# Every projection of a hybrid decoder block with the activations still in TensorE and 512 weight columns moving, two k-tiles a chunk

## The chip, the cores and the metric

One core of a Trainium2 chip. The metric is the device time of one execution in microseconds (us), median of three runs. The inputs are float32 in HBM, batch 1, 256 positions.

## The reference, cut to what matters

```python
u = rmsnorm(x, norm_w)                                   # (256, 4096)
proj = u @ w_in                                          # (4096, 24576)
(a_q, a_f, a_i, a_g, c_b, c_c, c_h, c_g, g_a, g_b) = split(proj)   # eight of 2048, two of 4096
f = lb + (1 - lb) * sigmoid(a_f);  k = 1 - f
o_a = rmsnorm(hgrn2(a_q, log(f), k, a_i), hgrn_norm_w)   # 16 heads of 128, linear recurrence
y_a = o_a * silu(a_g)
y_b = c_b * conv3(c_c * c_h) * silu(c_g)                 # causal, depthwise, 3 taps
merged = (sigmoid(g_a + bias_a) * (y_a @ w_branch_a)     # (2048, 4096)
          + sigmoid(g_b + bias_b) * (y_b @ w_branch_b))  # (2048, 4096)
out = rmsnorm(x + merged @ w_out, final_norm_w)          # (4096, 4096)
```

## The kernel before

**Arithmetic.** Each float32 operand of a projection is split in two: a high part (the value rounded to the type fp32r) and a low part (the rest). A product is high x high + high x low + low x high, summed in PSUM. The activations lie in `U` (`[128, 32 k-tiles, 256 high | 256 low]`), the branch outputs in `Y` in the same form.

**A unit of work** in this document is one k-tile (128 rows of a weight matrix) by 256 weight columns, for all 256 positions. There are 4096: 3072 for `w_in`, 512 for the two branch matrices, 512 for `w_out`. A unit is 1536 moving columns on TensorE, in both kernels.

**Two forms.** `channels` (L864) holds the weights still: for each of two 128-column blocks one matmul moves 512 columns (high and low activations against the high weights) and one moves 256 (high activations against the low weights). The result has channels on partitions. `positions` (L877, through `split_product`, L853) holds the activations still: for each of two blocks of 128 positions one matmul moves 256 weight columns (low activations, high weights) and one moves 512 (high activations, high and low weights). The result has positions on partitions. A unit is four matmuls and four weight loads in either form. `positions` serves the a_i group of the recurrence and `w_out`; all else is in `channels`.

**The chunk.** Weights come in chunks of 512 KB, four k-tiles by 256 columns, 1024 in all, 4 units each. Each passes SP (`load`, L225: one DMA into `RAW`), ScalarE (`hi`, L317, the instruction on L321: high part), VectorE (`lo`, L499, L501: low part) and TensorE. `RAW` and the split weights are rings of four. A load waits until the low part of the chunk four before is written; `hi` waits for its DMA and until TensorE has used the chunk four before (`w_used`); `lo` waits for `hi`; TensorE waits for `lo` (`lo_ready`). The split ring is placed at an offset in a 256-byte period that differs by stage: 192 bytes for the recurrence, 0 for the convolution, 128 for the merge, 64 for the output (`AT_...`); `U` lies at 0 and `Y` at 128.

**A group** is one output of 256 columns (eight chunks, or four for a branch matrix), into one of two double banks `PS0`, `PS1`. When it is done ScalarE copies the small halves out of PSUM (`small_half`, L323), VectorE adds them to the big halves (`drain_group`, L552) and multiplies by the 1/rms of x, which `x_rms` (L517) computes during the first group and a matmul with `ONES` (L948) spreads over the free axis. Group n+2 waits for the drain of group n.

**The order.** Eight recurrence iterations of four groups (a_f, a_q, a_i, a_g, two heads each), eight convolution iterations of four groups, sixteen merge iterations (g_a, g_b, z_a, z_b), sixteen output groups. The recurrence of iteration a runs in sixteen hand-written slots among the weight chunks of iteration a+1 (`attention`, on TensorE L886 with the level products on L906). The first group also transposes x (`turn_x`, L840, the instruction on L847: eight transposes before each chunk after the first) and makes `U` from it (L339, L508). The last group runs its last four chunks first for positions 0 to 127, then for 128 to 255, so that the final norm of the one half lies beside the other.

Of the kernel before, what the change touches and what calls it, by code (L numbers as in the profile page):

```python
# [18 lines left out]
KC = 4  # L41
# [3 lines left out]
NG = D // GW  # L45
XW = KC * P
XC = 1024
PERIOD = 256
AT_Y = 128
AT_HGRN, AT_CONV, AT_MERGE, AT_OUT = 192, 0, 128, 64  # L50
EARLY = 2
SLOTS = 16
# [3 lines left out]
A_Q, A_F, A_I, A_G, C_B, C_C, C_H, C_G = (BW * n for n in range(8))  # L56
G_A, G_B = 8 * BW, 8 * BW + D
HGRN_GROUPS = (A_F, A_Q, A_I, A_G)
CONV_GROUPS = (C_G, C_C, C_H, C_B)
X_AHEAD = ((4, 5), (6,), (7,), ())  # L60

TURNS_BRANCH = 4 * CD // RING
TURNS_MERGE = (2 * CD + 2 * CB) // RING
TURNS_OUT = 2 * CD // RING
CONV_TURN = NP * TURNS_BRANCH
MERGE_TURN = 2 * CONV_TURN
OUT_TURN = MERGE_TURN + NG * TURNS_MERGE
CONV_GROUP = 4 * NP
MERGE_GROUP = 2 * CONV_GROUP
OUT_GROUP = MERGE_GROUP + 4 * NG  # L70


def build(nc, x, norm_w, w_in, lb_logits, hgrn_norm_w, conv_w, w_branch_a, w_branch_b,
          gate_bias, w_out, final_norm_w, out):
    ctx = ExitStack()
    with ctx:
# [6 lines left out]
        def sem(name):  # L83
# [5 lines left out]
        region_y = region_u + KT * 2 * T * 4 + AT_Y  # L89
        region_m = region_y + 2 * KB * 2 * T * 4  # L90
# [6 lines left out]
        XR = at("XR", [P, 2, D], region_y + 2 * D * 4)  # L97
        MRG = at("MRG", [P, KT, T], region_m)
# [5 lines left out]
        ONES = at("ONES", [P, P], region_m + 8 * XW + 8 * P)  # L104
        VEC0 = at("VEC0", [KT, P], region_m + 8 * XW + 12 * P)
        W2 = 2 * T
        names = ["F", "V", "G", "SF", "SG", "PRE", "K", "SUF"]
        F, V, G, SF, SG, PRE, K, SUF = [at(n, [P, W2], region_m + 4 * W2 * i)
                                        for i, n in enumerate(names)]

        QX = at("QX", [P, 4, 192], region_m + 4 * W2 * len(names))
        QC = at("QC", [P, W2], region_m + 4 * W2 * len(names))
        scr = region_m + 4 * W2 * len(names) + 16 * 192
# [7 lines left out]
        RAW = [sb(f"RAW{i}", [P, KC, GW]) for i in range(RING)]  # L121
        ring = (nc.sbuf_base + PERIOD - 1) // PERIOD * PERIOD
        slot = KC * 2 * GW * 4 + PERIOD
        ctx.enter_context(nc.sbuf_tensor("ring", [P, (ring + RING * slot - nc.sbuf_base + 3) // 4], F32))

        def slots(stage, first):

            return [at(f"W{stage}{i}", [P, KC, 2 * GW], ring + i * slot + first, F32R) for i in range(RING)]

        W_HGRN, W_CONV = slots("H", AT_HGRN), slots("C", AT_CONV)  # L130
        W_MERGE, W_OUT = slots("M", AT_MERGE), slots("O", AT_OUT)
        SM = [sb(f"SM{i}", [P, 2, T]) for i in range(2)]
        GA, GB, Z = [sb(n, [P, W2]) for n in ("GA", "GB", "Z")]
        MASK = Z[:, 0:6 * 64]
        IDN = sb("IDN", [P, P])
        RB = sb("RB", [P, T])
        NW = GB[:, 64:64 + KT]
        VT1 = sb("VT1", [P, 96])
# [3 lines left out]
        LT = GB[:, 0:48]  # L142
        SSQ = sb("SSQ", [P, 2, NG])
# [5 lines left out]
        PS = [ctx.enter_context(nc.psum_tensor(f"PS{i}", [P, 2, 512], F32)) for i in range(2)]  # L149
# [8 lines left out]
        EPS_WRITTEN, IDN_WRITTEN, N_CONSTS = 1, 3, 19  # L158
# [6 lines left out]
        small_out = sem("small_out")  # L165
        drained = sem("drained")
        x_loaded = [sem(f"x_loaded{i}") for i in range(CD)]
# [8 lines left out]
        x_rstd = sem("x_rstd")  # L176
        x_spread = sem("x_spread")
# [6 lines left out]
        u_ready = sem("u_ready")  # L184
        gate_f = sem("gate_f")
        gate_g = sem("gate_g")
        level_ready = sem("level_ready")
# [6 lines left out]
        y_ready = sem("y_ready")  # L194
        merge_gate = sem("merge_gate")
        merged = sem("merged")
        m_hi = sem("m_hi")
        m_ready = sem("m_ready")
        xr_loaded = [sem(f"xr_loaded{i}") for i in range(2)]
        h_ready = sem("h_ready")  # L200
# [12 lines left out]

        block = ctx.enter_context(nc.Block())
# [3 lines left out]
        def _(sp):  # L218
# [12 lines left out]
            def column(i, col):  # L231


                return i * GW + col if col else (i + 1) * GW - GW

            def load_vectors():
                sp.dma_start(VEC1[0:32, :], lb_logits.rearrange("a (k p) -> (a k) p", p=P)).then_inc(vec_loaded, 16)
                sp.dma_start(VEC1[32:96, :], gate_bias.rearrange("a b (k p) -> (a b k) p", p=P)).then_inc(vec_loaded, 16)
# [3 lines left out]
            def branch(i, cols, turn0, first=False):  # L242
                for n, col in enumerate(cols):
                    col = column(i, col)
                    for c in range(CD):
                        if first and n == 0:
                            for j in ((c,) if c < RING else X_AHEAD[c - RING]):
                                load_x(j)
                            if c == CD - 1:
                                load_vectors()  # L250
                        load(w_in[0], c, col, turn0 + TURNS_BRANCH * i + (n * CD + c) // RING, c % RING,
                             free=not (first and n == 0 and c < RING))

            branch(0, HGRN_GROUPS, 0, first=True)
            with sp.Fori(1, NP) as i:
                branch(i, HGRN_GROUPS, 0)
            with sp.Fori(0, NP) as i:
                branch(i, CONV_GROUPS, CONV_TURN)
            with sp.Fori(0, NG) as i:
                turn = MERGE_TURN + TURNS_MERGE * i  # L260
                for n, col in enumerate((G_A, G_B)):
                    col = column(i, col)
                    for c in range(CD):
                        load(w_in[0], c, col, turn + (n * CD + c) // RING, c % RING)
                col = column(i, 0)
                for n, w in enumerate((w_branch_a, w_branch_b)):
                    for c in range(CB):
                        load(w[0], c, col, turn + (2 * CD + n * CB + c) // RING, c % RING)

            with sp.Fori(0, NG // 2) as i:  # L270
                for n in range(2):
                    col = column(i * 2 + n, 0)
                    for c in range(CD):
                        load(w_out[0], c, col, OUT_TURN + TURNS_OUT * i + (n * CD + c) // RING, c % RING)
                    if n == 0:
                        sp.wait_ge(w_used, RING * OUT_TURN)
                        sp.wait_ge(m_ready, CD)
                    cols = bass.ds(col, GW)
# [10 lines left out]
        def _(pool):  # L289
# [6 lines left out]
            pool.memset(ONES[:, :], 1.0).then_inc(consts, 1)  # L296
            pool.memset(AD[:, :, :], 0.0).then_inc(consts, 1)
            pool.memset(KL[:, :, :], 0.0).then_inc(consts, 1)
            pool.wait_ge(consts, 7)

            for n, m in enumerate(LEVELS[:6]):
# [3 lines left out]
                pool.wait_ge(consts, 8 + 2 * n)  # L305
# [6 lines left out]
        def _(act):  # L312
# [4 lines left out]
            def hi(ws, turn, s, free=True):  # L317
                act.wait_ge(raw_loaded[s], turn * 16 + 16)
                if free:
                    act.wait_ge(w_used, RING * turn + s - (RING - 1))  # L320
                act.activation(ws[s][:, :, 0:GW], RAW[s][:, :, :], ACT.Copy).then_inc(hi_ready, 1)  # L321

            def small_half(group, chunks, par, free=True, positions=False):  # L323
                act.wait_ge(w_used, chunks)
                if free:
                    act.wait_ge(drained, group - 1)
                if positions:
                    for b in range(2):
                        op = act.activation(SM[par][:, b, :], PS[par][:, b, T:2 * T], ACT.Copy, scale=ST[:, 12 + b:13 + b])
                    op.then_inc(small_out, 1)  # L330
                else:
                    act.activation(SM[par][:, :, :], PS[par][:, :, T:2 * T], ACT.Copy).then_inc(small_out, 1)

            act.wait_ge(gain_out, 1)
            for c in range(CD):

                for k in range(KC * c, KC * (c + 1)):
                    act.wait_ge(x_turned, k + 1)
                    act.activation(U[:, k, 0:T], XB[k % len(XB)], ACT.Copy, scale=NW[:, k:k + 1]).then_inc(u_hi, 1)  # L339
                hi(W_HGRN, c // RING, c % RING, free=c >= RING)  # L340

                act.wait_ge(x_loaded[c], 16)
                act.drain()
                act.activation(SQA[:, :], XS[:, 0, c * XW:(c + 1) * XW], ACT.Square,
                               accum_out=SSQ[:, 0, c:c + 1]).then_inc(x_sq, 1)
            def attention(a, slot):
                if slot == 1:

                    act.wait_ge(drained, 4 * a + 4)
                    act.activation(SG[:, :], G[:, :], ACT.Sigmoid).then_inc(gate_g, 1)  # L350
# [18 lines left out]
            def branch(i, turn0, group0, a=None, first=False, is_conv=False, after_it=None):  # L369
                own = W_CONV if is_conv else W_HGRN  # L370

                def ahead(c):

# [641 lines left out]
```

## Time and profile before

| | |
|---|---|
| median of 3 runs | 2955.69 us (2955.37 to 2956.11) |
| the profiled execution | 2955.83 us |
| its span | 2954.1 us |
| TensorE matmul busy | 2935.4 us (99%), 17061 matmuls |
| TensorE weight load busy | 2572.9 us (87%), 17061 loads |
| VectorE, ScalarE, GpSimd busy | 1700.8 us (58%), 1308.3 us (44%), 6.9 us |
| DMA | 552.32 MB, mean 187 GB/s, 60.4% of 16 engines' span |
| granted TensorE clock | 0.999 of full speed |

Busy time of a matmul is from its start to its modelled end, so that neighbours overlap; the spacing of their starts tells what one costs in a stream. In a timeline a row may hold several instructions (x2), with the time from the first's start to the last's end.

### The profile page before, as it was taken

What the parts mean: (1) busy time and instruction counts of PE and PEld (TensorE: products, weight loads), DVE (VectorE), ACT (ScalarE), POOL (GpSimd) and SP (SyncE); (2) the same over time, 40 slices, a digit from 0 to 9 for tenths busy, and PEclk for the clock granted to TensorE, in tenths of its full rate; (3) what the DMA queues carried; (4) which work ended last, traced back from release to release, by engine and by line L of the source; (5) the groups of instructions that cost most, each with busy time, mean ns of one, the idle gap of its engine ahead of it and who ended that gap; (6) DMA issues with size and microseconds to landing.
All of it is one profiled execution on the core that took longest, in us unless ns stands there. A gap on an engine that the chain in (4) does not pass through costs nothing.

```text
span 2954.1 us, 46544 instructions
## 1 busy us (share of the span) xinstructions
PE 2935.4 (99%) x17061; PEld 2572.9 (87%) x17061; DVE 1700.8 (58%) x1973; ACT 1308.3 (44%) x1523; POOL 6.9 (0%) x23
## 2 busy tenths in 40 slices
PE   9999999999999999999999999999999999999998
PEld 7888888888888888888888888888888888888887
DVE  7566665676665555555555555555555555655554
ACT  6444444444444444444444444444444444544444
POOL 0000000000000000000000000000000000000000
PEclk9999999999999999999999999999999999999999
DMA  7555555555556555566566666666666666666665
GB/s 242 180 177 166 171 176 177 165 172 174 173 171 191 187 190 186 179 196 192 186 191 186 190 186 190 185 191 186 190 186 190 186 190 186 189 203 208 202 204 190
DMA packets 550945, 552.32 MB, mean 187 GB/s; under 512 B 17217, under 2 KB 547826, under 8 KB 550898
## 3 DMA queue, kind: packets, MB, share of 16 engines
q1 hardware_dynamic: 550898, 551.71, 60.4%
q8 instruction: 27, 0.44, 0.1%
q14 instruction: 20, 0.16, 0.0%
HBM read 547.45 MB, written 4.19 MB: 187 GB/s over the span
## 4 chain that ended last, share of the span: by engine, by line
PE 99%; DMA 0%; DVE 0%; ACT 0%; issue 0%; ACTq 0%; SPq 0%; DVEq 0%
PE PS L869 52%; PE PS L872 26%; PE PS L861 12%; PE PS L856 6%; PE SC L906 1%; DMA XS<-in_x 0%; PE SS L906 0%; PE OB L915 0%; PE OB L916 0%; PE SC L896 0%; PE OB L914 0%; PE SS L921 0%; PE PS L847 0%; PE SC L847 0%; PE OB L847 0%
## 5 line engine op out<-in xcount | busy, mean ns | idle before, releaser
L501 DVE TENSOR_TENSOR WM<-RAW,WM 128x1024 fp32r<-128x1024 f32 x384 | 470.4, 1225 | 489.1 <-ACT WM L321 475.4
L321 ACT ACTIVATE WM<-RAW 128x1024 fp32r<-128x1024 f32 x384 | 407.5, 1061 | 605.1 <-PE PS L872 605.1
L869 PE MATMUL PS<-U,WC 128*128 128x512 f32 x2048 | 644.0, 396 | 0.0
L869 PE MATMUL PS<-U,WM 128*128 128x512 f32 x2048 | 638.0, 393 | 0.0
L869 PE MATMUL PS<-U,WH 128*128 128x512 f32 x1536 | 483.8, 396 | 0.5 <-DVE WH L501 0.5
L501 DVE TENSOR_TENSOR WC<-RAW,WC 128x1024 fp32r<-128x1024 f32 x256 | 312.2, 1225 | 282.9 <-ACT WC L321 273.7
L872 PEld LDWEIGHTS PS<-U,WC 128*128 128x128 f32 x2048 | 384.7, 188 | 90.9
L872 PEld LDWEIGHTS PS<-U,WM 128*128 128x128 f32 x2048 | 384.5, 188 | 89.2
L321 ACT ACTIVATE WC<-RAW 128x1024 fp32r<-128x1024 f32 x256 | 271.4, 1060 | 409.2 <-PE PS L872 409.2
L321 ACT ACTIVATE WH<-RAW 128x1024 fp32r<-128x1024 f32 x256 | 271.8, 1062 | 401.1 <-PE PS L872 273.4
L501 DVE TENSOR_TENSOR WH<-RAW,WH 128x1024 fp32r<-128x1024 f32 x256 | 311.6, 1224 | 227.8 <-ACT WH L321 217.4
L872 PE MATMUL PS<-U,WM 128*128 128x256 f32 x2048 | 406.1, 279 | 0.0
L872 PE MATMUL PS<-U,WC 128*128 128x256 f32 x2048 | 402.4, 278 | 0.0
L861 PE MATMUL PS<-WO,U 128*128 128x512 f32 x1024 | 359.1, 395 | 0.0
L872 PEld LDWEIGHTS PS<-U,WH 128*128 128x128 f32 x1536 | 289.0, 188 | 64.6
L869 PE MATMUL PS<-Y,WM 128*128 128x512 f32 x1024 | 321.4, 395 | 0.0
L869 PEld LDWEIGHTS PS<-U,WM 128*128 128x128 f32 x2048 | 312.8, 188 | 0.0
L869 PEld LDWEIGHTS PS<-U,WC 128*128 128x128 f32 x2048 | 311.8, 189 | 0.1
L872 PE MATMUL PS<-U,WH 128*128 128x256 f32 x1536 | 304.1, 279 | 0.0
L856 PE MATMUL PS<-WO,U 128*128 128x256 f32 x1024 | 285.5, 281 | 0.0
L501 DVE TENSOR_TENSOR WO<-RAW,WO 128x1024 fp32r<-128x1024 f32 x128 | 155.3, 1224 | 157.8 <-ACT WO L321 157.7
L869 PEld LDWEIGHTS PS<-U,WH 128*128 128x128 f32 x1536 | 234.5, 189 | 1.1 <-issue 0.7
(179 smaller groups left out, 2523.6 us busy)
## 6 DMA issues: line engine op xcount, KB each, us to landing
RAW<-in_w_in SPq DMA_DIRECT2D x768, 512.0 KB, 3.7
RAW<-in_w_out SPq DMA_DIRECT2D x128, 512.0 KB, 3.8
RAW<-in_w_branch_a SPq DMA_DIRECT2D x64, 512.0 KB, 3.7
RAW<-in_w_branch_b SPq DMA_DIRECT2D x64, 512.0 KB, 3.7
XS<-in_x SPq DMA_DIRECT2D x8, 512.0 KB, 9.7
XR<-in_x SPq DMA_DIRECT2D x16, 256.0 KB, 4.0
out_dram<-H SPq DMA_DIRECT2D x8, 512.0 KB, 4.0
FW<-in_final_norm_w SPq DMA_DIRECT2D x16, 128.0 KB, 3.8
```

The source lines that it names most:

```text
L321: act.activation(ws[s][:, :, 0:GW], RAW[s][:, :, :], ACT.Copy).then_inc(hi_ready, 1)
L501: dve.tensor_tensor(ws[s][:, :, GW:2 * GW], RAW[s][:, :, :], ws[s][:, :, 0:GW], ALU.subtract).then_inc(lo_ready, 1)
L856: return pe.matmul(bank[:, T:2 * T], stat_lo, both[:, 0:T], start=False, stop=stop, skip_group_check=True)
L861: op = pe.matmul(bank, stat_hi, both, start=first, stop=last, skip_group_check=True)
L869: pe.matmul(PS[par][:, t, :], w[:, k, t * P:(t + 1) * P], rhs[:, at_k, :], start=at_k == 0, stop=False, skip_group_check=True)
L872: op = pe.matmul(PS[par][:, t, T:2 * T], w[:, k, GW + t * P:GW + (t + 1) * P], rhs[:, at_k, 0:T], start=False, stop=at_k == n_tiles - 1, s ...
L906: op = pe.matmul(out, k_side, q_side, start=True, stop=True)
```

## The change

All projections take one form, `product`: the activations of 128 positions are still (`top` the high part, `low` the low part) and 512 weight columns move. One k-tile by 512 columns is six matmuls of 512 columns, three for each block of positions, and six weight loads. A chunk is two k-tiles by 512 columns: still 512 KB and 4 units, still 1024 chunks. In the branches its 512 columns are two blocks of 256 from two column groups (a_q and a_f, a_i and a_g; c_b and c_g, c_c and c_h), loaded by two DMAs of 256 KB. Groups are twice as wide: 2 in place of 4 in a branch iteration, 8 merge iterations and 8 output groups in place of 16.

Every result has positions on partitions. So 1/rms is one number for each partition (the `ONES` matmul, `RB` and `small_half` go), the merge biases are loaded by DMA broadcast to all partitions (`BIAS`), and what is needed with channels on partitions is transposed on TensorE: f and q after chunk 24 of each recurrence iteration (`turn_fq`), the gate product and c_c x c_h after chunk 2 of the next convolution iteration (`turn_conv`), and the merged output after chunk 3 of the next merge iteration (`turn_merged`), eight 128x128 transposes each, 192 in all. The ring of split weights lies at offset 0 of the period in all stages, with no padding between slots; so do `U` and `Y`.

```diff
-KC = 4
+OW = 512
+KC = 2
...
+FQ_AT, CONV_AT, MERGED_AT = 24, 2, 3
...
-            def load(w, rows, col, turn, s, free=True):
-                src = w[rows * KC * P:(rows + 1) * KC * P, bass.ds(col, GW)]
+            def load_pair(blocks, i, c, chunk, free=True):
+                s = c % RING
+                src = w_in[0][rows(c), 0:8 * BW].rearrange("(k p) (g c) -> p k g c", p=P, c=BW)
+                src = src[:, :, blocks, bass.ds((i + 1) * GW - GW, GW)]
                 if free:
-                    sp.wait_ge(lo_ready, RING * turn + s - (RING - 1))
-                sp.dma_start(RAW[s][:, :, :], src.rearrange("(k p) c -> p k c", p=P)).then_inc(raw_loaded[s], 16)
+                    sp.wait_ge(lo_ready, chunk - (RING - 1))
+                dst = RAW[s][:, :, :].rearrange("p k (g c) -> p k g c", g=2)
+                for k in range(KC):
+                    sp.dma_start(dst[:, k, :, :], src[:, k, :, :]).then_inc(raw_loaded[s], 16)
...
+            def load_bias(n, i):
+                cols = bass.ds((i + 1) * OW - OW, OW)
+                sp.dma_start(BIAS[:, :], gate_bias[0, n, cols].partition_broadcast(P)).then_inc(bias_loaded, 16)
...
-            def channels(par, w, rhs, k0, n_tiles):
-                for k in range(KC):
-                    at_k = k0 + k
-                    for t in range(2):
-                        pe.matmul(PS[par][:, t, :], w[:, k, t * P:(t + 1) * P], rhs[:, at_k, :],
-                                  start=at_k == 0, stop=False, skip_group_check=True)
-                    for t in range(2):
-                        op = pe.matmul(PS[par][:, t, T:2 * T], w[:, k, GW + t * P:GW + (t + 1) * P],
-                                       rhs[:, at_k, 0:T], start=False, stop=at_k == n_tiles - 1,
-                                       skip_group_check=True)
+            def product(par, s, left, k0, n_tiles, halves=(0, 1)):
+                w = WS[s]
+                for k in range(KC):
+                    at_k = k0 + k
+                    for b in halves:
+                        top, low = left[:, at_k, b * P:(b + 1) * P], left[:, at_k, T + b * P:T + (b + 1) * P]
+                        bank = PS[par][:, b, :]
+                        pe.matmul(bank, top, w[:, k, 0:OW], start=at_k == 0, stop=False)
+                        pe.matmul(bank, top, w[:, k, OW:2 * OW], start=False, stop=False)
+                        op = pe.matmul(bank, low, w[:, k, 0:OW], start=False, stop=at_k == n_tiles - 1)
                 return op
...
+            def turn_fq(i, first):
+                pe.wait_ge(drained, 2 * i + 1)
+                if first:
+                    pe.wait_ge(lb_ready, 1)
+                blocks = [GA[:, b, h * P:(h + 1) * P] for h in range(4) for b in range(2)]
+                for g in range(4):
+                    pe.transpose(SC[1][:, g * P:(g + 1) * P], blocks[g], IDN[:, :])
+                turn(SC[0], blocks[4:], fq_turned)
+            def turn_conv(a):
+                pe.wait_ge(drained, CONV_GROUP + 2 * a + 2)
...
+            def turn_merged(i):
+                pe.wait_ge(merged, i + 1)
...
-            def drain_group(dst, group, par, norm=None):
...
+            def scaled(dst, src):
+                for b in range(2):
+                    op = dve.tensor_scalar(dst[:, b, :], src[:, b, :], inv_rms(b), None, ALU.mult)
+                return op
...
                     if c == 2 * CD + CB - 1:
+                        dve.wait_ge(w_used, chunk + c + 1)
+                        dve.wait_ge(merge_gate, 2 * i + 1)
+                        dve.tensor_tensor(GA[:, :, :], PS[0][:, :, :], GA[:, :, :], ALU.mult).then_inc(drained, 1)
+                dve.wait_ge(w_used, chunk + MERGE)
+                dve.wait_ge(merge_gate, 2 * i + 2)
+                dve.tensor_tensor(GB[:, :, :], PS[1][:, :, :], GB[:, :, :], ALU.mult).then_inc(drained, 1)
+                after()
+                dve.tensor_tensor(GA[:, :, :], GA[:, :, :], GB[:, :, :], ALU.add).then_inc(merged, 1)
```

## Rows read from the trace of the kernel before

**Rows 1.** The page: busy time of each engine, and the granted clock in 40 slices
```profile
PE 2935.4 (99%) x17061; PEld 2572.9 (87%) x17061; DVE 1700.8 (58%) x1973; ACT 1308.3 (44%) x1523; POOL 6.9 (0%) x23
...
PEclk9999999999999999999999999999999999999999
```

**Rows 2.** The page: the chain that ended last, by engine, shares of the span
```profile
PE 99%; DMA 0%; DVE 0%; ACT 0%; issue 0%; ACTq 0%; SPq 0%; DVEq 0%
```

**Rows 3.** Waits: engine, line, who was waited for: total us, times, longest
```profile
ACT WM L321 <- PE PS L872: 605.1, 383, 2.0
DVE WM L501 <- ACT WM L321: 475.4, 319, 1.8
...
SPq L229 <- DVE WM L501: 839.9, 384, 5.6
```

**Rows 4.** Windows, TensorE alone, in convolution, merge, output: stretch, length, busy (matmuls), clock
```profile
900.00:1470.00 570.00, 570.00 (x3275) 1.00 0.60 189
1490.00:2570.00 1080.00, 1080.00 (x6201) 1.00 0.62 188
2590.00:2930.00 340.00, 340.00 (x1936) 1.00 0.67 204
```

**Rows 5.** Timeline of TensorE in a recurrence iteration, channels form: start, us, instructions
```profile
85.64 0.62 PE L869 MATMUL PS<-U,WH 128*128 128x512 f32 x2
...
88.40 0.39 PE L869 MATMUL PS<-U,WH 128*128 128x512 f32 x1
```

**Rows 6.** Timeline of TensorE, positions form, in a recurrence iteration
```profile
171.85 0.40 PE L861 MATMUL PS<-WH,U 128*128 128x512 f32 x1
172.08 0.28 PE L856 MATMUL PS<-WH,U 128*128 128x256 f32 x1
172.20 0.40 PE L861 MATMUL PS<-WH,U 128*128 128x512 f32 x1
...
173.26 0.40 PE L861 MATMUL PS<-WH,U 128*128 128x512 f32 x1
```

**Rows 7.** The same form in the output stage
```profile
2637.94 0.39 PE L861 MATMUL PS<-WO,U 128*128 128x512 f32 x1
...
2639.33 0.40 PE L861 MATMUL PS<-WO,U 128*128 128x512 f32 x1
```

**Rows 8.** Groups by line: weight loads; timeline: two of them side by side
```profile
L872 PEld LDWEIGHTS PS<-U,WC 128*128 128x128 f32 x2048 | 384.7, 188 | 90.9
```
```profile
86.22 0.30 PEld L869 LDWEIGHTS PS<-U,WH 128*128 128x128 f32 x2
```

**Rows 9.** Timeline of TensorE in the first group: one chunk with eight transposes of x
```profile
15.38 0.71 PE L869 MATMUL PS<-U,WH 128*128 128x512 f32 x2
...
19.04 0.70 PE L869 MATMUL PS<-U,WH 128*128 128x512 f32 x2
```

**Rows 10.** Groups by line on VectorE and ScalarE: busy, mean ns of one, idle before
```profile
L501 DVE TENSOR_TENSOR WM<-RAW,WM 128x1024 fp32r<-128x1024 f32 x384 | 470.4, 1225 | 489.1 <-ACT WM L321 475.4 <-issue 9.7
L321 ACT ACTIVATE WM<-RAW 128x1024 fp32r<-128x1024 f32 x384 | 407.5, 1061 | 605.1 <-PE PS L872 605.1
...
L332 ACT ACTIVATE SM<-PS 128x512 f32<-128x512 f32 x135 | 78.1, 579 | 0.0
L565 DVE TENSOR_TENSOR SM<-PS,SM 128x512 f32<-128x512 f32 x88 | 60.6, 689 | 10.6 <-issue 7.4 <-ACT SM L332 2.0
```

**Rows 11.** Timeline of the first 50 us: making of U, a stall, the ONES matmul
```profile
6.88 0.90 ACT L339 ACTIVATE U<-SC,GB 128x256 fp32r<-128x256 f32 x2
```
```profile
37.18 0.70 PE L869 MATMUL PS<-U,WH 128*128 128x512 f32 x2 [0.53 <-DVE WH L501]
```
```profile
45.92 0.70 PE L948 MATMUL SC<-GA,ONES 128*128 128x256 f32 x2
```

**Rows 12.** Timeline of VectorE behind the last matmul
```profile
2942.96 0.42 DVE L815 TENSOR_TENSOR GB<-PS,SM 128x256 f32<-128x256 f32 x1
2943.89 0.42 DVE L817 CUSTOM_DVE_ANT_0 SM<-GB 128x256 f32<-128x256 f32 x1 [0.50 <-issue]
```

**Rows 13.** The page, DMA issues: count, KB each, us to landing
```profile
RAW<-in_w_in SPq DMA_DIRECT2D x768, 512.0 KB, 3.7
```

More of the change, by code:

```diff
@@ L315, in _, with hi @@
             act.activation(ST[:, 19:20], EPT[:, :], ACT.Sqrt)
-            def hi(ws, turn, s, free=True):
-                act.wait_ge(raw_loaded[s], turn * 16 + 16)
+            def hi(chunk, s, free=True):
+                act.wait_ge(raw_loaded[s], (chunk - s) * (16 * KC // RING) + 16 * KC)
                 if free:
[L320 to L332, printed above, removed]
+                    act.wait_ge(w_used, chunk - (RING - 1))
+                act.activation(WS[s][:, :, 0:OW], RAW[s][:, :, :], ACT.Copy).then_inc(hi_ready, 1)
             act.wait_ge(gain_out, 1)
@@ L399, in branch @@
                         gates(i)
-                    if slot % 4 == 3:
-                        n = slot // 4
-                        small_half(group0 + 4 * i + n, RING * (turn0 + TURNS_BRANCH * i) + CD * (n + 1), n % 2, free=not (first and n < 2), positions=n == 2 and not is_conv)
-            branch(0, 0, 0, first=True)
-            with act.Fori(1, NP - 1) as i:
-                branch(i, 0, 0, a=i - 1)
-            branch(NP - 1, 0, 0, a=NP - 2, after_it=W_CONV)
-            branch(0, CONV_TURN, CONV_GROUP, a=NP - 1, is_conv=True)
@@ new lines, in branch @@
+                    if is_conv and slot == 15:
+                        act.wait_ge(w_used, chunk0 + BRANCH * i + 2 * CD)
+                        act.wait_ge(drained, CONV_GROUP + 2 * i + 1)
+                        for b in range(2):
+                            op = act.activation(pair(SF)[:, b, :], PS[1][:, b, 0:T], ACT.Copy, scale=inv_rms(b))
+                        op.then_inc(gate_c, 1)
+            branch(0, 0, first=True)
+            with act.Fori(1, NP) as i:
+                branch(i, 0, a=i - 1)
@@ new lines, in _, with merge @@
+            branch(0, CONV_CHUNK, a=NP - 1, is_conv=True)
+            with act.Fori(1, NP) as i:
+                branch(i, CONV_CHUNK, is_conv=True)
+            def merge(i, first=False, last=False):
+                chunk = MERGE_CHUNK + MERGE * i
+                group = MERGE_GROUP + 4 * i
+                for c in range(MERGE):
+                    hi(chunk + c + RING, c % RING)
+                    if not first and c == MERGED_AT + 2:
+                        act.wait_ge(m_turned, i)
+                        for j in range(2):
+                            op = act.activation(MRG[:, bass.ds(i * 4 + 2 * j - 4, 2), :], pair(SC[j]), ACT.Copy)
+                        op.then_inc(m_kept, 1)
+                    if c in (CD + 1, 2 * CD + 1):
@@ L950, in branch @@
-            def branch(i, turn0, group0, modes, a=None, first=False):
-                for n in range(4):
-                    group(W_HGRN if turn0 == 0 else W_CONV, turn0 + TURNS_BRANCH * i, n * CD, CD, modes[n], U, 0, n % 2, group0 + 4 * i + n,
-                          free=not (first and n < 2), u_wait=(u_ready, KC) if first and n == 0 else None, a=a)
-            hgrn = (channels, channels, positions, channels)
-            branch(0, 0, 0, hgrn, first=True)
+                    pe.wait_ge(lo_ready, chunk0 + at_chunk + 1)
@@ new lines, in group, with branch, between @@
+                    product(par, at_chunk % RING, left[:, k_start:k_start + n_chunks * KC, :], c * KC,
+                            n_chunks * KC).then_inc(w_used, 1)
+                    between(at_chunk)
+            def branch(i, chunk0, group0, a=None, first=False, is_conv=False, conv_of=None):
+                def between(c):
+                    if a is not None:
+                        attention(a, c)
+                    if first and c == CD + 1:
+                        turn_vectors()
+                    if not is_conv and c == FQ_AT:
+                        turn_fq(i, first)
+                    if conv_of is not None and c == CONV_AT:
+                        turn_conv(conv_of)
+                for n in range(2):
+                    group(chunk0 + BRANCH * i, n * CD, CD, U, 0, n, group0 + 2 * i + n, between,
+                          free=not first, x_first=first and n == 0)
@@ new lines, in merge, with between @@
+            def merge(i, first=False):
+                def between(c):
+                    if first and c == CONV_AT:
+                        turn_conv(NP - 1)
+                    if not first and c == MERGED_AT:
+                        turn_merged(i - 1)
+                chunk0, g = MERGE_CHUNK + MERGE * i, MERGE_GROUP + 4 * i
+                group(chunk0, 0, CD, U, 0, 0, g, between)
+                group(chunk0, CD, CD, U, 0, 1, g + 1, between)
+                pe.wait_ge(y_ready, 2 * NP)
+                group(chunk0, 2 * CD, CB, Y, 0, 0, g + 2, between)
+                group(chunk0, 2 * CD + CB, CB, Y, KB, 1, g + 3, between)
@@ L970, in output @@
+            merge(0, first=True)
+            with pe.Fori(1, NM) as i:
+                merge(i)
             def output(i, first=False, last=False):
                 for n in range(1 if last else 2):
-                    group(W_OUT, OUT_TURN + TURNS_OUT * i, n * CD, CD, positions, U, 0, n, OUT_GROUP + 2 * i + n,
-                          u_wait=(m_ready, 1) if first and n == 0 else None)
+                    pe.wait_ge(drained, OUT_GROUP + 2 * i + n - 1)
+                    for c in range(CD):
+                        if first and n == 0 and c % 2 == 0:
+                            pe.wait_ge(m_ready, c // 2 + 1)
+                        at_chunk = OUT_CHUNK + 2 * CD * i + n * CD + c
+                        pe.wait_ge(lo_ready, at_chunk + 1)
+                        product(n, c % RING, U, c * KC, KT).then_inc(w_used, 1)
+                        if first and n == 0 and c == MERGED_AT:
+                            pe.wait_ge(m_kept, NM - 1)
+                            turn_merged(NM - 1)
```

620 lines of the change are left out of this document (290 added, 330 removed).

## The prediction

> **What bounds the kernel now.** I read the page first: TensorE is busy for 99% of the span at full clock, VectorE for 58%, ScalarE for 44% [rows 1]. A matmul's end is modelled, so 99% alone proves little. The chain that ended last says more: 99% of it is TensorE [rows 2]. The waits then show that everything else waits for TensorE: in the merge stage ScalarE waits 605.1 us until TensorE frees a slot of split weights, VectorE 475.4 us for ScalarE, SP 839.9 us for VectorE [rows 3]. Preparation follows the matmuls; it doesn't hold them up. So the question is how closely matmul starts follow one another.
>
> A unit (one k-tile by 256 weight columns) is 1536 moving columns; at one column a cycle of the granted 2.4 GHz it would take 640 ns. Four matmuls make a unit, so the windows give 4 x 570/3275 = 696 ns in the convolution, 4 x 1080/6201 = 697 in the merge, 4 x 340/1936 = 702 in the output stage [rows 4]. Recurrence, weights still: one chunk of four units from 85.64 to 88.40 is 2.76 us, 690 ns a unit [rows 5]. Positions form: four pairs (two units) take 1.41 us in the recurrence, 705 a unit [rows 6], and 1.39 us here in the output stage, 695 [rows 7]. Summed by their numbers: 768 x 0.690 + 256 x 0.705 + 1024 x 0.696 + 1536 x 0.697 + 512 x 0.702 = 2853 us. The other 101 us of the span are the recurrence's own products, the transposes, the start, small waits and the tail.
>
> **The stream.** The change removes no moving column: 3 matmuls of 512 in place of two of 512 and two of 256. What can change is the excess of 50 to 65 ns a unit over 640. It has two possible prices. By column, the unit stays as it is: 695 to 705 in the form that holds activations still. By instruction, three quarters of the excess stay: from the positions mean of 702 that is 640 + 0.75 x 62 = 687, from the quickest row, 690, it is 677.5. The single starts lie between the two: a 512 takes 0.23 us (171.85 to 172.08), a 256 takes 0.12 [rows 6], against 0.213 and 0.107 by column count; the excess of a 512 is larger, but not twice as large. No row has three 512s one after another with the same activations still, so this is an estimate with both ends kept: 677.5 to 707 (705 and 2 ns for the rounding of the rows). I take 0.232 us for a 512, 696 ns a unit, because the nearest rows, the positions form, put their 512s at 0.23. Stream: 4096 x 0.696 = 2851, **-2 us**.
>
> The trace has a 256 following in 0.12 us while a weight load lasts 188 ns, two loads side by side fitting into 0.30 us [rows 8]; loads overlap and don't set the spacing, and four loads or three a unit is all one. The Trainium skill, Perfetto Trace Analysis (Identifying the Most-Contended Engine), takes the load's busy share as the better measure of how near TensorE is to its limit; by that rule 87% is the bound and a quarter fewer loads would free time. The trace speaks against it here. The skill's page TensorE: Matmul & The Clock Gate (Wait — 56ns, not 53.3ns?) gives N/2.4 + about 2.5 ns between starts, 215.8 ns for a 512; then a unit would be 650 before and 647.5 after, an estimate of -10 us from fewer instructions. The rows, at 0.23, don't follow it.
>
> **Transposes.** 24 places of eight, on TensorE's path. The price is in the first group: a chunk with eight transposes of x lasts 15.38 to 19.04 = 3.66 us, one without 2.76 [rows 5, 9], so eight cost 0.90. 24 x 0.90 = **+21.6 us**. They can't be hidden, since TensorE is the bound. Bounds: nothing if they run in gaps (there are none), 48 us at twice the price. The transposes of x and the recurrence's products stay.
>
> **Start.** The first product needs two k-tiles of `U` rather than four: one ScalarE pair of 0.90 us less before the first `hi` [rows 11]; I take -0.8. The 0.53 us stall ahead of the eighth chunk goes, since per chunk ScalarE has half the `U` work; the `ONES` matmul goes [rows 11], 0.6 net of the vector transposes that stay. **-1.9 us**. The first group now fetches 12 MB over sixteen chunks where it was 8 MB over eight, but at 3.2 us or more a chunk; the DMA engines are not the limit there.
>
> **Tail.** Behind the last matmul one add of 512 stands for two of 256, and the square sum is 512 wide (0.69 for 0.42) [rows 10, 12]: **+0.2 us**.
>
> **Costed at nothing, with their cover.** Chunk, `hi` and `lo` keep their size: 1061 and 1225 ns in 2.78 us [rows 10]. Between the freeing of a slot and its use there are three chunks, 8.3 us; `hi` and `lo` take 2.3, so 6 us of slack cover what is put among them. The drains: the `small_half` copies (135 x 579 ns) and one add (88 x 689) go [rows 10], wide operations of 1024 elements come, about 1.2 us each; at the end of a merge iteration VectorE does two in a row, 2.5 us, inside the slack. The new waits of TensorE: `turn_merged` comes after four chunks, 11.1 us, and its chain is `hi` and `lo` 2.3 + 2.5 + drains, under 6; `turn_conv` comes after three chunks, 8.3 us, with a chain of `hi`, two ScalarE copies, two VectorE products, under 5; `turn_fq` waits for a group drained eight chunks before. If one were late, every chunk behind it would start late, since TensorE's queue is in order; but the queues behind VectorE and ScalarE still have the slack. DMA: the bytes stay; branch chunks are two issues of 256 KB in place of one. Landing takes 3.7 us [rows 13] and starts when `lo` frees the slot four chunks ahead, so about 5 us remain. The bias loads (16 of 256 KB written) stand in SP's queue behind waits that are long fulfilled. If that cover failed, one chunk would be late by what is missing, seldom over 2 us, in 16 places.
>
> **Sum.** 2954.1 - 2 + 21.6 - 1.9 + 0.2 = 2972 for the span; 1.7 us lie around the span (2955.83 - 2954.1), the profiled execution being within 0.2 of the median: about **2973 us**.
>
> **The rivals.**
> 1. *Fewer instructions pay* (the other side): the excess belongs to the matmul, a 512 takes 0.229 us. Unit 687: 4096 x 0.687 = 2814, -39, +19.9 for the rest: 2936 us; at 677.5 it is 2897. It decides from 692 ns a unit (0.2306 us for a 512), where the stream gains 20 us and pays for the transposes. For it: a 256 carries 12 ns more than its columns, more than half of a 512's. Against: the positions form, nearest to the new one, is the dearest. Chance 0.27.
> 2. *Full rate*: three equal matmuls in a row stream at one column a cycle of 2.4 GHz, unit 640: 2621, -232, +19.9: 2744 us. Against: no stage comes near it. The skill's load measure and its 2.5 ns rule would lead here. Chance 0.04.
> 3. *The dear form everywhere*: all at 705 to 707, as in rows 6, because weights move and `U` is the still operand, or because the ring lies at one offset with `U`: +35 to +43 on the stream, 3010 to 3018 us. For it: the spacing differs by stage (690 to 705) with nothing but form and place of the operands different. Chance 0.22.
> 4. *A turn comes too early* or a drain delays a chunk: 24 places at 1 us, 2997 us. Against: the slack above. Chance 0.07.
>
> My forecast, 0.40: unit of 692 to 701.
>
> **How the numbers follow.** A measurement of this kernel can tell 0.2%, 6 us, from no change. Faster: rivals 1 and 2 and the low edge of the forecast, 0.33. Within 0.2% (units of 691 to 693.5): 0.12. Slower: 0.55. The range leaves out rival 2 and the ends of 1 and 3: 2915 to 3012. Both signs carry weight, so the forecast alone: 2956 to 2993.
>
> **What would show it.** All groups of matmuls are 128x512 but for the recurrence; 12288 of them, starts 0.232 apart; a chunk of 2.78 us in every stage. Three groups of 64 transposes, idle before them near nothing. ScalarE still waits for TensorE, VectorE for ScalarE. The prediction is wrong if a 512 follows in under 0.2306 us (faster), if chunks differ by stage, if TensorE shows idle time before the transposes, or if its waits name a DMA.

## The result and the profile after

| | before | after |
|---|---|---|
| median | 2955.9 us | 2910.4 us (2910.26 to 2911.84) |
| ratio | | 0.9847, interval 0.983 to 0.9864 |
| span of the profiled execution | 2954.1 us | 2908.5 us |
| matmuls, weight loads | 17061 | 13155 |

The change makes the kernel 1.5% faster, 45.5 us. I had forecast 2973 us, slower, with 2915 to 3012 as range: wrong in direction, and just outside the range. (The median before is now that of four runs.)

The page of the changed kernel, busy times, clock and chain, in the form of [rows 1, 2]:

```profile
PE 2889.1 (99%) x13155; PEld 2399.5 (82%) x13155; DVE 1600.1 (55%) x1794; ACT 1231.9 (42%) x1326; POOL 6.7 (0%) x22
...
PEclk9999999999999999999999999999999999999999
...
PE 99%; DVE 0%; ACT 0%; DMA 0%; ACTq 0%; DVEq 0%; issue 0%; SPq 0%
```

TensorE is still the whole chain. Who waits for whom is unchanged too, against [rows 3]:

```profile
ACT WS L314 <- PE PS L839: 1613.6, 957, 3.1
DVE WS L483 <- ACT WS L314: 1226.6, 868, 2.9
...
SPq L222 <- DVE WS L483: 1061.0, 512, 4.3
```

So the gain is in the spacing of matmuls, and the timeline shows it. This is TensorE in the convolution, one matmul a row, start first:

```profile
986.18 0.39 PE L839 MATMUL PS<-WS,U 128*128 128x512 f32 x1
986.41 0.39 PE L837 MATMUL PS<-WS,U 128*128 128x512 f32 x1
986.63 0.39 PE L838 MATMUL PS<-WS,U 128*128 128x512 f32 x1
986.86 0.39 PE L839 MATMUL PS<-WS,U 128*128 128x512 f32 x1
987.09 0.39 PE L837 MATMUL PS<-WS,U 128*128 128x512 f32 x1
987.31 0.39 PE L838 MATMUL PS<-WS,U 128*128 128x512 f32 x1
...
990.03 0.39 PE L838 MATMUL PS<-WS,U 128*128 128x512 f32 x1
```

From 987.31 to 990.03 are twelve matmuls, one chunk of four units: 2.72 us, 0.2267 a matmul, 680 ns a unit. Before, a chunk took 2.76 to 2.82 us, by stage [rows 4 to 7]. The same stretch of the output stage, where nothing else runs on TensorE, counts matmuls, before and then after:

```profile
2660.00:2860.00 200.00, 200.00 (x1140) 1.00 0.68 205
```
```profile
2660.00:2860.00 200.00, 200.00 (x884) 1.00 0.66 212
```

Four of 175 ns make a unit of 702 ns before, three of 226 make 679 after. (A count over 200 us is good to one or two matmuls.)

The turns, here between two chunks of the convolution, with the matmul before and behind:

```profile
888.50 0.39 PE L839 MATMUL PS<-WS,U 128*128 128x512 f32 x1
888.73 0.60 PE L899 MATMUL SC<-IDN,F 128*128 128x128 f32 x4
889.17 0.60 PE L845 MATMUL SC<-IDN,SG 128*128 128x128 f32 x4
889.52 0.48 PE L837 MATMUL PS<-WS,U 128*128 128x512 f32 x1
889.84 0.40 PE L838 MATMUL PS<-WS,U 128*128 128x512 f32 x1
```

No idle time stands before the transposes. They take 0.79 us to the start of the next matmul, and that one is followed after 0.32 in place of 0.23: 0.9 us in all, as forecast.

At the start TensorE now waits before the first product, and later it has two stalls where there was one [rows 11]:

```profile
9.45 0.76 PE L837 MATMUL PS<-WS,U 128*128 128x512 f32 x1 [2.01 <-DVE WS L483]
...
59.31 0.47 PE L837 MATMUL PS<-WS,U 128*128 128x512 f32 x1 [0.23 <-DVE WS L483]
...
62.92 0.51 PE L837 MATMUL PS<-WS,U 128*128 128x512 f32 x1 [0.60 <-DVE WS L483]
```

### The profile page after: what moved, and what is told of

It reads as the page before. It is cut to its first block, busy times and chain, and to the rows that moved or that the text cites. A ratio compares the mean times of both kernels' runs of the same rounds, so it can differ in the third digit from the quotient of the medians.

```text
span 2908.5 us, 39078 instructions
## 1 busy us (share of the span) xinstructions
PE 2889.1 (99%) x13155; PEld 2399.5 (82%) x13155; DVE 1600.1 (55%) x1794; ACT 1231.9 (42%) x1326; POOL 6.7 (0%) x22
## 4 chain that ended last, share of the span: by engine, by line
PE 99%; DVE 0%; ACT 0%; DMA 0%; ACTq 0%; DVEq 0%; issue 0%; SPq 0%
PE PS L837 32%; PE PS L839 32%; PE PS L838 32%; PE SC L868 1%; PE SC L845 0%; PE SS L868 0%; DMA XS<-in_x 0%; DVE WS L483 0%; PE SS L845 0%; PE OB L878 0%; PE OB L877 0%; PE SC L858 0%; PE OB L876 0%; PE SC L899 0%; PE SC L891 0%; PE SC L907 0%
## 5 line engine op out<-in xcount | busy, mean ns | idle before, releaser
L483 DVE TENSOR_TENSOR WS<-RAW,WS 128x1024 fp32r<-128x1024 f32 x1024 | 1253.7, 1225 | 1247.9 <-ACT WS L314 1226.6
L314 ACT ACTIVATE WS<-RAW 128x1024 fp32r<-128x1024 f32 x1024 | 1084.6, 1060 | 1617.4 <-PE PS L839 1613.6
L837 PE MATMUL PS<-WS,U 128*128 128x512 f32 x3584 | 1408.2, 393 | 2.8 <-DVE WS L483 2.8
L839 PE MATMUL PS<-WS,U 128*128 128x512 f32 x3584 | 1397.3, 390 | 0.0
L838 PE MATMUL PS<-WS,U 128*128 128x512 f32 x3584 | 1396.7, 390 | 0.0
L839 PEld LDWEIGHTS PS<-WS,U 128*128 128x128 f32 x3584 | 673.5, 188 | 140.9
L837 PEld LDWEIGHTS PS<-WS,U 128*128 128x128 f32 x3584 | 673.8, 188 | 140.0 <-issue 3.0
L838 PEld LDWEIGHTS PS<-WS,U 128*128 128x128 f32 x3584 | 674.0, 188 | 135.8
L839 PE MATMUL PS<-WS,Y 128*128 128x512 f32 x512 | 199.4, 389 | 0.0
L837 PE MATMUL PS<-WS,Y 128*128 128x512 f32 x512 | 199.4, 389 | 0.0
L838 PE MATMUL PS<-WS,Y 128*128 128x512 f32 x512 | 199.3, 389 | 0.0
L839 PEld LDWEIGHTS PS<-WS,Y 128*128 128x128 f32 x512 | 96.1, 188 | 20.0
L838 PEld LDWEIGHTS PS<-WS,Y 128*128 128x128 f32 x512 | 96.1, 188 | 19.9
L837 PEld LDWEIGHTS PS<-WS,Y 128*128 128x128 f32 x512 | 96.2, 188 | 19.9
L868 PEld LDWEIGHTS SC<-QR,KL 128*126 128x126 f32 (+5 forms) x384 | 42.9, 173 | 6.4 <-issue 2.8
L868 PE MATMUL SC<-QR,KL 128*126 128x64 f32 (+5 forms) x384 | 42.5, 254 | 0.0
L565 DVE TENSOR_TENSOR PRE<-PRE 128x256 f32<-128x256 f32 x56 | 23.9, 426 | 4.6 <-issue 0.5
L553 DVE TENSOR_TENSOR KL<-K,SUF 128x256 f32<-128x256 f32 x56 | 23.3, 416 | 0.0
```

Source lines behind the costliest of these rows:

```text
L314: act.activation(WS[s][:, :, 0:OW], RAW[s][:, :, :], ACT.Copy).then_inc(hi_ready, 1)
L483: dve.tensor_tensor(WS[s][:, :, OW:2 * OW], RAW[s][:, :, :], WS[s][:, :, 0:OW], ALU.subtract).then_inc(lo_ready, 1)
L553: op = dve.tensor_tensor(halves(KL[:, n % 2, :], m)[0], halves(K[:, :], m)[0], s_left, ALU.mult)
L565: dve.tensor_tensor(p_right, p_right, over_left, ALU.mult)
L837: pe.matmul(bank, top, w[:, k, 0:OW], start=at_k == 0, stop=False)
L838: pe.matmul(bank, top, w[:, k, OW:2 * OW], start=False, stop=False)
```

## The experiments

Theories: **I**, a matmul with its weight load costs a constant over its columns; **C**, the excess goes by columns; **R**, a second matmul on the same still operand is cheaper; **P**, the place of the split ring against `U` sets the excess; **M**, neighbours of unequal size cost. The kernel before was timed beside every run; the ratios are to it. e13 was timed once, the others four times or more. No run leaves out any of the work.

### e1: the old mix of sizes in the new form

```diff
-                        op = pe.matmul(bank, low, w[:, k, 0:OW], start=False, stop=at_k == n_tiles - 1)
+                        for c0 in (0, 256):
+                            op = pe.matmul(bank[:, c0:c0 + 256], low, w[:, k, c0:c0 + 256], start=False,
+                                           stop=at_k == n_tiles - 1, skip_group_check=True)
```

> The changed kernel with one edit: the low x high matmul of 512 columns is issued as two of 256, so that a unit is again two matmuls of 512 and two of 256, as before the change. Theory I (the excess over one column a cycle belongs to the matmul with its weight load, 13 ns each): 4096 more matmuls cost 55 us, about 2965 us, a chunk of four units goes from 2.72 to 2.77 us. Theory C (the excess goes by moving columns, and something else in the change, place or order, made the columns cheaper): no change, about 2910 us, chunk 2.72 us.

Measured: 2975.6 us, ratio to before 1.0068 (1.0051 to 1.0084); 65.2 us more than the changed kernel. The timeline in the convolution, and below it the kernel before at the same time:

```profile
1305.51 0.40 PE L843 MATMUL PS<-WS,U 128*128 128x512 f32 x1
1305.74 0.39 PE L844 MATMUL PS<-WS,U 128*128 128x512 f32 x1
1305.97 0.40 PE L839 MATMUL PS<-WS,U 128*128 128x256 f32 x2
1306.20 0.40 PE L843 MATMUL PS<-WS,U 128*128 128x512 f32 x1
...
1307.60 0.40 PE L843 MATMUL PS<-WS,U 128*128 128x512 f32 x1
```
```profile
1306.17 0.63 PE L869 MATMUL PS<-U,WC 128*128 128x512 f32 x2
1306.64 0.39 PE L872 MATMUL PS<-U,WC 128*128 128x256 f32 x2
1306.87 0.40 PE L869 MATMUL PS<-U,WC 128*128 128x512 f32 x1
```

1306.20 to 1307.60 are two units, 0.70 each; before, 1306.17 to 1306.87 is one, 0.70. With the ring at offset 0 the new form with the old sizes runs as the old form did. C falls. This one edit takes back more than the whole gain: the number and size of the matmuls are worth 65 us, and which operand is still shows no price in these rows. Theory I had said 55 us, 13.3 ns for each of the 4096 matmuls more; it was 15.9. So about 10 us of the 65 come with the mixture of sizes and not with the count; no run says why.

### e2: the same still operand not twice in a row

The third and the second matmul of `product` change places.

> The changed kernel with the three matmuls in the order high x high, low x high, high x low, so that no two neighbours hold the same activations still. Theory I: no change, 2910 us, 0.227 us for each matmul. Theory R (a second matmul on the same still operand is cheaper, which the order before the change could not use): the two cheap successions of six go, each costing up to the 4 to 5 ns by which a 512 got cheaper, 12288 x 5 = up to 60 us, about 2970 us.

Measured: 2910.6 us (0.9847, 0.983 to 0.9863). R falls: loading the same operand twice in succession saves nothing.

### e3, e6, e7, e12, e15, e14: the ring moved against U

```diff
-        region_w = region_y + 2 * KB * 2 * T * 4
+        region_w = region_y + 2 * KB * 2 * T * 4 + 64
```

and 128, 192, 32, 96, 256 in the others.

e3, 64 bytes:

> The changed kernel with the ring of split weights, RAW and what lies behind them moved by 64 bytes against U and Y, the offset that the output stage had before the change. Theory I: no change, 2910 us. Theory P (the place of the ring against U sets the excess): the spacing moves from 0.227 towards the 0.230 to 0.235 of the kernel before, 12288 x 3 to 8 ns = 37 to 98 us more, 2947 to 3008 us.

e6, 128 bytes:

> The changed kernel with the ring of split weights 128 bytes off against U in the 256-byte period. Theory P2 (what counts is the place of the moving operand against the still one; 64 bytes cost 6.75 ns a unit, 25.6 us in all): another chunk length than 2.720 and 2.747 us, either way, by up to some 30 us. If the merge stage of before is a guide, where 128 bytes gave 697 ns against 697 at 0, nothing changes: 2910 us.

e7, 192 bytes:

> The changed kernel with the ring 192 bytes off against U. In the recurrence stage of before 192 bytes gave 690 ns a unit against 696.7 at 0 (the run of before with all offsets at 0). Theory P2: a gain of up to 27 us, 2883 us, if the offset works alike in the form with 512 columns alone; no change or a loss if not.

e12, 32 bytes:

> The changed kernel with the ring 32 bytes off against U. At 0, 64, 128, 192 bytes a unit takes 680, 687, 697, 700 ns. On the line between 0 and 64: 683 to 684, 2922 us. If offset 0 is no optimum but one point of a curve, it could fall under 680, to 2900 us or less.

e15, 96 bytes:

> The changed kernel with the ring 96 bytes off against U. Measured: 2910 at 0, 2989 at 32, 2936 at 64, 2979 at 128, 2988 at 192. If 0 and 64 are the two good places and odd multiples of 32 the bad ones: near 2989 us. A time under 2910 would show that 0 is no floor.

e14, 256 bytes:

> The changed kernel with the ring, RAW and what lies behind them 256 bytes further off from U. If the place matters within a period of 256 bytes: 2910 us, chunk 2.720 us. If the distance itself matters: another time, up to the 2989 us of 32 bytes.

| offset, bytes | 0 | 32 | 64 | 96 | 128 | 192 | 256 |
|---|---|---|---|---|---|---|---|
| us | 2910.4 | 2989.2 | 2936.1 | 2988.5 | 2979.3 | 2988.4 | 2911.1 |
| ratio to before | 0.9847 | 1.0112 | 0.9934 | 1.0111 | 1.008 | 1.011 | 0.9849 |

The intervals are about 0.0017 to either side. The stretch 2660 to 2860 us, at 64, 128 and 192 bytes:

```profile
2660.00:2860.00 200.00, 200.00 (x876) 1.00 0.65 207
```
```profile
2660.00:2860.00 200.00, 200.00 (x862) 1.00 0.64 206
```
```profile
2660.00:2860.00 200.00, 200.00 (x859) 1.00 0.64 204
```

884 matmuls at offset 0 become 876, 862 and 859: 0.226, 0.228, 0.232 and 0.233 us each. P holds, and is larger than the whole effect of the change: with the ring 32, 96, 128 or 192 bytes off the new kernel would have been 0.8 to 1.1% slower than the old. 256 is as good as 0, so it is the place within a period that counts. Several expectations were wrong. For 64 bytes I had at least 37 us more, it was 26. For 128 I had up to 30 us either way, it was 69 more; for 192 a gain or some loss, it was 78 more: the old stages at these offsets (697 and 690 ns a unit) were no guide. For 32 bytes I had a line from 0 to 64: the price isn't smooth, and 64 is the cheapest place but 0 of those tried. None of the five other places tried in the period beats 0; 160 and 224 bytes were not tried.

### e9, e10: what against what

```diff
-        base = (nc.sbuf_base + PERIOD - 1) // PERIOD * PERIOD
+        base = (nc.sbuf_base + PERIOD - 1) // PERIOD * PERIOD + 128
```

> The changed kernel with the whole arena 128 bytes further: U, Y, the split ring, RAW and the rest keep their places against one another. If the place of the ring against U counts (relative), 2910 us, chunk 2.720 us. If the ring's own place in the period counts (absolute), as in the run with 128 bytes: 2979 us, chunk 2.79 us.

Measured: 2910.9 us (0.9847, 0.9831 to 0.9863). In e10 the ring alone moves by 128 bytes, and RAW and the scratch return to offset 0:

```diff
+        region_w = region_y + 2 * KB * 2 * T * 4 + 128
+        region_r = region_w + RING * KC * 2 * OW * 4 + 128
```

> The changed kernel with only the split ring 128 bytes off; RAW and all behind it are back at offset 0 of the period. If TensorE's reads of the ring against those of U make the difference, 2979 us, chunk 2.79 us, as with everything behind U and Y moved. If RAW or the scratch against U had done it, 2910 us.

Measured: 2980.9 us (1.0083, 1.0066 to 1.01), as in e6. The place is relative, and it is that of the ring TensorE moves against the `U` and `Y` it holds still.

### e4: the kernel before with all at offset 0

`AT_Y` and all four ring offsets are set to 0.

> The kernel before with the split ring and Y at offset 0 of the 256-byte period in all stages, as after the change. Theory I: the number of matmuls is unchanged, so the time stays within 10 us of 2956. Theory P: it falls by what the change won on the stream, 64 us, to about 2892 us.

Measured: 2955.6 us (1.0, 0.999 to 1.0009). The 2892 us of theory P was wrong. The stages moved against each other. In the recurrence the channels form lost what 192 bytes had given it: this row pair and its distance, four units, is 2.80 us against 2.76 [rows 5].

```profile
86.16 0.64 PE L869 MATMUL PS<-U,WH 128*128 128x512 f32 x2
...
88.96 0.40 PE L869 MATMUL PS<-U,WH 128*128 128x512 f32 x1
```

The output stage won a little (1145 matmuls from 2660 to 2860 us where there were 1140, 699 ns a unit for 702). With the old sizes, then, no gain from offset 0; place and size act together.

### e5 and e13: smaller matmuls

Every matmul but the first of a sum is issued in two of 256 columns, or in four of 128.

> The changed kernel with every projection matmul issued as two of 256 columns (save the first of each sum), six a unit. Theory I (a fixed excess for each matmul with its load): from the mixed run a 256 costs 0.1216 us when a 512 costs 0.2267, so a unit is 6 x 0.1216 = 0.730 us, chunk 2.92 us, 205 us more than the changed kernel: about 3115 us. Theory M (only neighbours of unequal size cost): all are equal again, chunk about 2.72 us, 2910 us.

> The changed kernel with every projection matmul issued as four of 128 columns (save the first of each sum), twelve a unit. By columns plus a constant of 13.3 ns, a matmul of 128 takes 66.7 ns, a unit 800 ns, 4096 x 0.120 = 492 us more than the changed kernel, about 3400 us, plus waits at the loop ends as with 256 columns. If a weight load sets a floor of 120 ns for each matmul, a unit takes 1440 ns, about 6000 us in all.

e5 measured: 3124.6 us (1.0571, 1.0553 to 1.0588). A stretch of it in the merge:

```profile
1800.00:1870.00 70.00, 70.00 (x582) 1.00 0.60 189
```

70/582 = 0.120 us a matmul, 720 ns a unit. From 256 to 512 columns the spacing grows from 120.0 to 226.7 ns: 106.7 ns for 256 columns, one a cycle of 2.4 GHz, with 13.3 ns left over both times. As the cause of the change M falls, since all are equal here and the unit is 40 ns dearer. 4096 x 0.040 = 164 us of the 214 are this. The rest is mostly waits that I hadn't expected, and a lower clock behind them:

```profile
PE PS L844 <- issue: 18.1, 8, 2.4
PE PS L844 <- DVE WS L483: 13.2, 6, 2.8
PE PS L839 <- issue: 10.0, 6, 2.8
```
```profile
1884.50:1888.00 3.50, 3.50 (x18) 0.58 0.58 175
```

Two of these twenty waits are those of the start. The other eighteen, 38 us in all, stand at the turns of the recurrence loop (twelve, two at each turn) and of the merge loop (six), whose bodies have here nearly twice the matmuls; the convolution loop has none. In fourteen of them TensorE waits for nothing that the profile shows. The last row above follows a turn of the merge loop, where TensorE had waited 2.26 us until 1884.33: the granted clock was 0.58 over 3.5 us, and 0.94 over the next four. Over the run the clock is 0.994 where it was 0.999, about 15 us by estimate. The changed kernel has no wait at a loop's turn. Its DMA queue for instructions moved 33 packets, that of e5 182 and that of e13 430 (part 3 of their pages), so the waits may be for the instructions themselves; no run tests that.

e13 gave 7578 us in one run. Its page, with the clock in 40 slices, one wait, and windows before and behind it:

```profile
PE 7518.9 (99%) x49587; PEld 7504.6 (99%) x49587; DVE 1602.7 (21%) x1794; ACT 1234.2 (16%) x1326; POOL 6.7 (0%) x22
...
PEclk9998888889965555555555557998898898997555
```
```profile
2157.61 0.79 PE L844 MATMUL PS<-WS,U 128*128 128x512 f32 x1 [2.90 <-DVE WS L483]
```
```profile
2100.00:2150.00 50.00, 50.00 (x450) 1.00 0.33 103
2200.00:4600.00 2400.00, 2400.00 (x11224) 0.50 0.17 52
4660.00:4700.00 40.00, 40.00 (x360) 1.00 0.34 99
```

The expectation of 6000 us by a floor was near in kind. At full clock, in the 10 us from 949.83 on, 92 matmuls are about 0.112 us apart, far from 0.067. So 128 columns meet a floor of about 0.112 us that isn't their columns. Weight loads are busy for 99% of the span and are the likely cause, but no run changes the loads alone. At 256 columns the loads are busy for 98% too (3050.9 of 3122.2 us in e5); 0.120 lies above the floor, yet so little that a part of its 13.3 ns may belong to the load.

The rest of the time is the clock. From 2200 to 4600 us it is at its lower level, 1.2 GHz, and a matmul takes 0.214 us. After the start TensorE waits fourteen times, 2.5 to 3.1 us each, at loop turns, and the granted clock falls to 0.50 behind each of the fourteen and nowhere else. It came back after 40 to 55 us in twelve cases, after 2500 us in the one shown, and not before the end behind the wait at 6914 us, while TensorE issued without a gap. (From 100 to 400 us the record has the clock at 1.00 and 1403 matmuls, also 0.214 us each, so the record is not to be trusted there.) By estimate some 19,000 matmuls had the slower pace, 0.10 us each: 1900 to 2000 us, which with 48720 x 0.112 us and some 120 us of other work comes near the 7578.

### e11: alternate banks

The six matmuls of a k-tile are ordered high x high for both halves of positions, then high x low, then low x high.

> The changed kernel with the six matmuls of a k-tile ordered so that the two banks alternate: high x high for both halves of positions, then high x low, then low x high. Same matmuls, same sums. If part of the 13.3 ns that each matmul takes over its columns comes from following in the same bank, the spacing falls from 0.2267 towards 0.2133, up to 164 us less. If it belongs to the matmul with its load, no change: 2910 us. The still operand now changes at every matmul; the order with the low part in the middle showed that as free.

Measured: 2910.5 us (0.9846, 0.9829 to 0.9862). No part of the 13.3 ns comes from following in the same bank.

### e8: the turns doubled

```diff
+                if done is not o_turned:
+                    for n in range(8):
+                        g = n % 4
+                        op = pe.transpose(bank[:, g * P:(g + 1) * P], blocks[g], IDN[:, :])
                 op.then_inc(done, 1)
```

> The changed kernel with the 24 turns of eight transposes doubled: eight more transposes of blocks already turned, into the same bank, behind the eight. (They overwrite blocks of the second bank with the blocks of that bank's first four, so its contents stay.) If turns lie on TensorE's path at 0.90 us for eight, 24 x 0.87 to 0.90 = 21 to 22 us more, 2932 us. If part of them hides in waits, less; if they disturb the queues of VectorE and ScalarE, more.

Measured: 2931.7 us (0.9916, 0.99 to 0.9933), +21.3 us. The turns lie wholly on TensorE's path.

## Why the prediction was wrong, point by point

- **What bounds the kernel**: right. TensorE is 99% of the chain before and after, and all that stood under "costed at nothing" stayed hidden: no wait before a turn, none for a drain, ScalarE's waits for weights from DMA 3.7 us in all.
- **The stream**: the step that failed. I took 0.232 us for a 512-column matmul, 696 ns a unit, -2 us; it takes 0.2267, 680 ns: 4096 x 0.680 = 2785 against 2853, **-68 us**. Both bounds, 677.5 and 707, were wide enough; the choice between them was not. I took it from the nearest form. But those rows had two things that the new kernel lacks: the ring 192 or 64 bytes off against `U`, and 256-column matmuls between the 512s. e1 shows what the sizes are worth at offset 0 (65 us), e3, e6, e7, e12 and e15 what the place is worth with equal sizes (26 to 79 us). The prediction had named the sign itself: a 512 that follows in under 0.2306 us.
- **Column or instruction**: the excess belongs to the matmul. With equal sizes at offset 0 it is 13.3 ns for 512 and for 256 columns alike. A matmul and its load come together in every run, so the price can't be divided between them. "Three quarters stay" from the 56 ns of the convolution would have been 42; 40 stay.
- **The single starts misled me.** A 512 at 0.23 and a 256 at 0.12 looked like an excess that grows with the columns. But the rows are rounded to 0.01 us, 10 ns, and the question was one of 5: in e1 the same 0.23 and 0.12 are printed, and a pure 0.2267 and 0.120 would be printed so too. Only the sum over a unit or a long window is fine enough, and it holds for its own mixture alone.
- **The two rules of the Trainium skill.** TensorE: Matmul & The Clock Gate (Wait — 56ns, not 53.3ns?) has columns over 2.4 GHz plus a constant. The form is right at offset 0: 226.7 and 120.0 ns are columns plus 13.3 both times. The size isn't: the page has about 2.5, from bf16 matmuls, and these are float32r. Its 647.5 ns a unit, taken for the new kernel alone, is near rival 2's 640, and 680 refutes both. The load's busy share, the measure of Perfetto Trace Analysis (Identifying the Most-Contended Engine), fell from 87 to 82% with the time. I had said that the trace speaks against it; that was too strong. Fewer loads did free time, but the matmuls went down with them, and the share is 98% in e5 and 99% in e13, where a floor showed. No run tells whether the share or the count of matmuls is what mattered.
- **Transposes**: +21.6 forecast, 21.3 by e8. Right. (The bound "at twice the price" is 43 us, not 48.)
- **Start and tail**: -1.7 forecast. The sum -68 + 21.6 = -46.4 against -45.6 of the spans leaves about +1, so this small term was off by some 3 us. The first product is 0.9 us earlier (9.45 for 10.36 us), as forecast. But TensorE idles 2.01 us before it, where the kernel before was turning x; in place of one stall of 0.53 us come two of 0.83 together; and x is turned in fourteen interruptions of four transposes where there were six of eight. Four cost 0.46 us (two matmuls and a turn from 13.63 to 14.54), 6.4 us in all against 5.4.
- **The rivals.** Rival 1 had the mechanism, with 0.27; the gain in its 2936 us was too small, and 2910 lies between its two figures, 2897 and 2936. The measured 0.2267 us is on its side of the deciding point, 0.2306. Rival 3 named one offset of the ring with `U` as a danger; the place matters, but that offset is the good one. At 32, 96, 128 and 192 bytes the kernel is inside my 2956 to 2993 (2979 to 2989), which is luck: I had not reckoned with the place. No run came to the 3010 of rival 3. The chance of faster, 0.33, rested on taking "nearest form" for "nearest condition".

**Open:** what the 13.3 ns are made of (not the bank, not the change of still operand; matmul and load were never varied apart), why a mixture of sizes costs 10 us more than the count, and why the place of the moving operand against the still one changes them. That a load's reads and the moving reads meet would fit, but no run separates them.

## What to carry to other kernels

Where matmuls follow one another without a gap, count instructions as well as columns: with float32r operands, each weight load with its matmul cost 13 ns over its columns at best (512 and 256 columns; at 128 it was 58), so fewer and wider matmuls pay even if no column is saved. Try the place of the moving operand against the still one in steps of 32 bytes over 256 before judging such a change; here that alone moved the time by 2.7%. And price an operation in a stream by the sum over a whole repeat, at the same place and mix, not by one gap that is printed to 10 ns.

## What the runs showed of the hardware that I had not expected

- Moving one buffer by 32 bytes against the other operand of TensorE cost 78.8 us of 2910 (e12), with no wait in the profile: only the spacing grows. 256 bytes cost nothing (e14), and moving both by 128 costs nothing (e9).
- With 128 columns a matmul (e13), each of fourteen waits of 2.5 to 3.1 us was followed by half the clock, and TensorE, issuing without a gap, did not get it back for 40 to 55 us, once for 2500 us (0.50 from 2200 to 4600 us, 0.214 us a matmul). Behind a wait of 2.26 us with 256 columns (e5) the clock was 0.58 over 3.5 us and 0.94 over the next four.
- With nearly twice the matmuls in a loop body TensorE waited 2 to 3 us at the turn of two of the loops, mostly for nothing that the profile shows (e5).
